# Up projection of a feed-forward block, steps 3 to 10: the weights' high part against both token parts in one 512-column product

## The reference, cut to what matters

```python
D_MODEL, SEQ, FFN_HIDDEN, FFN_CONV = 1024, 256, 2816, 3
...
h = h + merged @ w_out
hid = causal_dwconv(rms_norm(h, ffn_norm_g) @ w_ffn_up, ffn_conv_w, ffn_conv_b)
g_ff, up = jnp.split(hid, 2, axis=-1)
return h + (jax.nn.silu(g_ff) * up) @ w_ffn_down
...
return rms_norm(h, final_norm_g)
```

## Time and profile before

| | us |
|---|---|
| median of 3 runs | 750.46 (750.32 to 751.18) |
| span of the profiled execution | 752.8 |
| TensorE busy in it | 704.3 |
| VectorE busy in it | 529.6 |
| ScalarE busy in it | 345.1 |

### The profile page before, as it was taken

How to read it: one execution, slowest core, us unless ns; L and a number is a source line. 1 busy time by engine, 2 the same in 40 slices (tenths; PEclk the granted TensorE clock), 3 DMA queues, 4 the chain that set the end, 5 groups by cost and what they waited for, 6 DMA issues and landing times.

```text
span 752.8 us, 13896 instructions
## 1 busy us (share of the span) xinstructions
PE 704.3 (94%) x5478; PEld 684.3 (91%) x5478; DVE 529.6 (70%) x614; ACT 345.1 (46%) x397; POOL 98.9 (13%) x56
## 2 busy tenths in 40 slices
PE   5599968979798999999999999999999999999994
PEld 5599967979798999999999999999999999999993
DVE  3789967989967465667664544566559877777784
ACT  5436416445463444544543333443355644555542
POOL 2735320413247000000000000000000000000021
PEclk9889988999999999999999999999999999999998
DMA  8619559464853554334346675655435656555511
GB/s 267 184 47 347 111 85 328 120 211 123 283 180 96 168 167 158 122 119 155 125 161 181 196 237 174 201 183 195 147 133 175 216 177 202 178 171 201 185 56 56
DMA packets 118280, 128.40 MB, mean 171 GB/s; under 512 B 4302, under 2 KB 113263, under 8 KB 117743
## 3 DMA queue, kind: packets, MB, share of 16 engines
q1 hardware_dynamic: 118255, 128.04, 53.9%
HBM read 125.37 MB, written 2.65 MB: 170 GB/s over the span
## 4 chain that ended last, share of the span: by engine, by line
PE 69%; DVE 13%; issue 6%; SPq 5%; POOL 2%; ACT 2%; DMA 2%; DVEq 0%; POOLq 0%; ACTq 0%
PE ps L337 22%; PE ps L338 22%; PE ps L339 22%; DVE conv_a L1169 4%; DVE w_lo L309 3%; SPq L291 3%; DMA w_raw<-w_in 2%; SPq L283 1%; POOL mem_nat L1529 1%; DVE dt_w L1131 1%; DVE conv_g L1439 1%; POOL mem_nat L1531 1%; POOL stat L1486 1%; ACT w_hi L305 1%; PE ps L377 1%
## 5 line engine op out<-in xcount | busy, mean ns | idle before, releaser
L337 PE MATMUL ps<-tok_hi,w_hi 128*128 128x256 f32 x1056 | 306.1, 290 | 6.7 <-DVE w_lo L309 3.6
L338 PE MATMUL ps<-tok_lo,w_hi 128*128 128x256 f32 x1056 | 302.7, 287 | 0.0
L339 PE MATMUL ps<-tok_hi,w_lo 128*128 128x256 f32 x1056 | 302.6, 287 | 0.0
L309 DVE TENSOR_TENSOR w_lo<-w_raw,w_hi 128x2048 fp32r<-128x2048 f32 x102 | 236.7, 2321 | 69.6 <-ACT w_hi L305 69.3
L305 ACT ACTIVATE w_hi<-w_raw 128x2048 fp32r<-128x2048 f32 x108 | 206.0, 1908 | 66.1 <-PE ps L339 48.7
L337 PEld LDWEIGHTS ps<-tok_hi,w_hi 128*128 128x128 f32 x1056 | 207.3, 196 | 9.9 <-issue 5.5
L338 PEld LDWEIGHTS ps<-tok_lo,w_hi 128*128 128x128 f32 x1056 | 207.1, 196 | 0.4
L339 PEld LDWEIGHTS ps<-tok_hi,w_lo 128*128 128x128 f32 x1056 | 206.6, 196 | 0.0
L1169 DVE SCALAR_TENSOR_TENSOR conv_a<-pad_x,cols_conv,conv_a 128x256 f32<-128x256 f32 x72 | 67.2, 999 | 3.4 <-ACT pad_x L873 3.3
L309 POOL TENSOR_TENSOR w_lo<-w_raw,w_hi 128x2048 fp32r<-128x2048 f32 x6 | 28.0, 4673 | 186.4 <-ACT w_hi L305 186.4
L879 ACT ACTIVATE tanh_a<-conv_a 128x512 f32<-128x512 f32 x12 | 7.6, 631 | 72.5 <-DVE conv_a L1169 72.5
(11 more groups left out here) (276 smaller groups left out, 1230.0 us busy)
## 6 DMA issues: line engine op xcount, KB each, us to landing
w_raw<-w_in SPq DMA_DIRECT2D x95, 512.0 KB, 4.8
w_raw<-w_ffn_up SPq DMA_DIRECT2D x44, 512.0 KB, 4.4
w_raw<-w_ffn_down SPq DMA_DIRECT2D x22, 512.0 KB, 4.1
w_raw<-w_mem_kv SPq DMA_DIRECT2D x16, 512.0 KB, 4.1
w_raw<-w_br_ssm SPq DMA_DIRECT2D x16, 512.0 KB, 4.2
acs_b<-acs_d SPq DMA_DIRECT2D x4, 1024.0 KB, 8.1
w_raw<-w_br_attn SPq DMA_DIRECT2D x8, 512.0 KB, 4.6
w_raw<-w_br_mem SPq DMA_DIRECT2D x8, 512.0 KB, 4.0
```

The costliest lines, as they stand in the source:

```text
L309: dve.tensor_tensor(w_lo[:, s, :], w_raw[:, s, :], w_hi[:, s, :].bitcast(F32), ALU.subtract).then_inc(lo_ready[s], 1)
L337: pe.matmul(o, a[0], b[0], start=start, stop=False, **kw)
L338: pe.matmul(o, a[0], b[1], start=False, stop=False, **kw)
L339: return pe.matmul(o, a[1], b[0], start=False, stop=stop, **kw)
```

## The change

From step `F_WIDE` = 3 on, eight of the eleven steps, the up projection is computed otherwise:

- The tokens are scaled once: VectorE multiplies what was turned into banks 4 to 7 by the gain and by `rstd_b` into `normed` (`normalise`, 8 operations of 256 columns). ScalarE makes the high part (`norm_high`, 4 operations of 512 columns) and VectorE the low part (`norm_low`, 4 of 512 columns). Both lie side by side in `hn`, 256 columns of high part and 256 of low part for each depth tile.
- `gemm_wide` takes the place of `gemm_cols`: the high part of the weights meets high and low part of the tokens in one product of 512 columns that fills a whole bank, and the low part of the weights meets the high part of the tokens in one of 256 columns that adds into the bank's second half. The block of a slot now needs two banks, 0 and 1 for the gate and 2 and 3 for up. The result is the sum of a bank's two halves.
- To take a block, ScalarE first copies the second halves of both banks into `pad_g` or `pad_u`, and VectorE then adds the first halves (in place of the product with `rstd_b`).
- `normalise` stands on VectorE behind step 0, `norm_high` on ScalarE behind step 0, `norm_low` on VectorE behind step 1. Steps 1 and 2 are written out and compute as before. As `normalise` reads banks 4 to 7, the four zero products move behind the up block of step 1, with a wait for all 8 operations of `normalise`, ahead of the first down block.

```diff
--- before.py
+++ after.py
@@ -64,6 +64,7 @@
 BIAS_W = 3 * P
 
 RA, RB, RC, RD, RE, RF, RG = 0, 8, 12, 16, 20, 24, 26
+F_WIDE = 3
 
 
 def constants():
@@ -207,6 +208,8 @@
     last_hi = place("last_hi", R + 20, [2, T], F32R)
     last_lo = place("last_lo", R + 22, [2, T], F32R)
     rstd_b = place("rstd_b", R + 18.5, [T])
+    normed = place("normed", R + 72, [KT, T])
+    hn = place("hn", R + 56, [KT, 2, T], F32R)
     pad_g = place("pad_g", R + 0, [2, FTAPS - 1 + T])
     pad_u = place("pad_u", R + 2.25, [2, FTAPS - 1 + T])
     conv_g = place("conv_g", R + 4.5, [2, T])
@@ -268,6 +271,7 @@
     x_again, late_gain, h_sumsq, h_var, h_rstd, h_spread, rstd_b_ready, h_turned, h_hi, h_lo = map(
         sem, ("x_again", "late_gain", "h_sumsq", "h_var", "h_rstd", "h_spread", "rstd_b_ready", "h_turned", "h_hi",
               "h_lo"))
+    n_step, n_hi, n_lo, crossed = map(sem, ("n_step", "n_hi", "n_lo", "crossed"))
     pads_zero, conv_begun, f_step, g_tanh, g_silu, hid_done, hid_hi_s, hid_lo_s = map(
         sem, ("pads_zero", "conv_begun", "f_step", "g_tanh", "g_silu", "hid_done", "hid_hi_s", "hid_lo_s"))
     down_done, y_added, y_sumsq, y_var, y_rstd, y_scaled, y_out = map(
@@ -337,6 +341,24 @@
         pe.matmul(o, a[0], b[0], start=start, stop=False, **kw)
         pe.matmul(o, a[0], b[1], start=False, stop=False, **kw)
         return pe.matmul(o, a[1], b[0], start=False, stop=stop, **kw)
+
+    def gemm_wide(pe, r, s):
+
+        pe.wait_ge(lo_ready[s], r + 2)
+        pe.wait_ge(bank_free[s], r + 1)
+        for j in range(2):
+            b = 2 * s + j
+            for k in range(KT):
+                w = slice(k * CW + j * P, k * CW + (j + 1) * P)
+                if k:
+                    pe.matmul(ps[:, b, T:2 * T], w_lo[:, s, w], hn[:, k, 0, :], start=False, stop=False,
+                              skip_group_check=True)
+                mm = pe.matmul(halves(b), w_hi[:, s, w], hn[:, k, :, :], start=k == 0, stop=k == KT - 1,
+                               skip_group_check=True)
+                if k == 0:
+                    pe.matmul(ps[:, b, T:2 * T], w_lo[:, s, w], hn[:, k, 0, :], start=False, stop=False,
+                              skip_group_check=True)
+        mm.then_inc(gemm_done[s], 1)
 
     def rows_part(pe, s, t, ks, hi, lo, start, stop, **kw):
 
@@ -819,16 +841,32 @@
                         mm = pe.matmul(ps[:, 3, t * P:(t + 1) * P], stat[:, 4 + t:5 + t].to_broadcast([P, P]), ident,
                                        start=True, stop=True)
                     mm.then_inc(h_spread, 1)
-                    for b in range(4, 8):
-                        open_bank(pe, b)
-            with pe.Fori(1, F_STEPS) as f:
-                r = f + (RG - 1)
-                gemm_cols(pe, r, 0, tok_hi, tok_lo)
-                gemm_cols(pe, r, 1, tok_hi, tok_lo)
+
+            def down(r, f):
+
                 pe.wait_ge(hid_lo_s, f)
                 pe.wait_ge(lo_ready[2], r + 2)
                 down_part(pe, 2, 0, hid_hi, hid_lo)
                 down_part(pe, 2, 1, hid_hi, hid_lo).then_inc(gemm_done[2], 1)
+
+            for f in range(1, F_WIDE):
+                r = f + (RG - 1)
+                gemm_cols(pe, r, 0, tok_hi, tok_lo)
+                gemm_cols(pe, r, 1, tok_hi, tok_lo)
+                if f == 1:
+                    pe.wait_ge(n_step, KT)
+                    for b in range(4, 8):
+                        open_bank(pe, b)
+                down(r, f)
+            pe.wait_ge(n_lo, KT // 2)
+            pe.wait_ge(bank_free[1], RG + F_WIDE)
+            pe.wait_ge(bank_free[2], RG + 1)
+            pe.wait_ge(rstd_b_ready, 1)
+            with pe.Fori(F_WIDE, F_STEPS) as f:
+                r = f + (RG - 1)
+                gemm_wide(pe, r, 0)
+                gemm_wide(pe, r, 1)
+                down(r, f)
             pe.wait_ge(hid_lo_s, F_STEPS)
             pe.wait_ge(lo_ready[0], RG + F_STEPS + 1)
             for t in range(NT):
@@ -1026,8 +1064,13 @@
             split_hi(act, RG, 0)
 
 
-            def ffn(f, sa, ra, sb, rb, after_gate, after_up, last, first=False, final=False):
+            def ffn(f, sa, ra, sb, rb, after_gate, after_up, last, first=False, final=False, wide=False):
                 for n, (s, r, pad, conv, tile) in enumerate(((sa, ra, pad_g, conv_g, 0), (sb, rb, pad_u, conv_u, FT))):
+                    if wide:
+                        act.wait_ge(gemm_done[s], r + 1)
+                        act.wait_ge(f_step, 8 * f - 4 + 4 * n)
+                        act.activation(pad[:, :, FTAPS - 1:], ps[:, 2 * s:2 * s + 2, T:2 * T],
+                                       ACT.Copy).then_inc(crossed, 1)
                     act.wait_ge(bank_free[s], r + 2)
                     if not first:
                         act.wait_ge((g_silu, hid_done)[n], f)
@@ -1048,12 +1091,22 @@
                 for rr, ss in last:
                     split_hi(act, rr, ss)
 
+            def norm_high():
+
+                act.wait_ge(n_step, KT)
+                for k in range(0, KT, 2):
+                    act.activation(hn[:, k:k + 2, 0, :], normed[:, k:k + 2, :], ACT.Copy).then_inc(n_hi, 1)
+
             ffn(0, 1, RF + 1, 2, RF + 1, [(RG, 1)], [(RG, 2)], [], first=True)
-            with act.Fori(1, F_STEPS - 1) as f:
+            norm_high()
+            for f in range(1, F_WIDE):
                 r = f + (RG - 1)
                 ffn(f, 0, r, 1, r, [(r + 1, 0)], [(r + 1, 1)], [(r + 1, 2)])
+            with act.Fori(F_WIDE, F_STEPS - 1) as f:
+                r = f + (RG - 1)
+                ffn(f, 0, r, 1, r, [(r + 1, 0)], [(r + 1, 1)], [(r + 1, 2)], wide=True)
             r = RG + F_STEPS - 2
-            ffn(F_STEPS - 1, 0, r, 1, r, [(r + 1, 0)], [], [], final=True)
+            ffn(F_STEPS - 1, 0, r, 1, r, [(r + 1, 0)], [], [], final=True, wide=True)
             for n in range(2 * NT):
                 act.wait_ge(y_added, n + 1)
                 act.activation(h_sc[:, n // 2, halfcols(n)], h_nat[:, n // 2, halfcols(n)], ACT.Square,
@@ -1419,12 +1472,32 @@
             dve.wait_ge(pads_zero, 2)
 
 
-            def ffn(f, sa, ra, sb, rb, early, after_gate, after_up, final=False):
+            def normalise():
+
+                for k in range(KT):
+                    dve.scalar_tensor_tensor(normed[:, k, :], ps[:, 4 + k // 2, (k % 2) * T:(k % 2 + 1) * T],
+                                             cols_gate[:, 5 * KT + k:5 * KT + k + 1], rstd_b[:], ALU.mult,
+                                             ALU.mult).then_inc(n_step, 1)
+
+            def norm_low():
+
+                for k in range(0, KT, 2):
+                    dve.wait_ge(n_hi, k // 2 + 1)
+                    dve.tensor_tensor(hn[:, k:k + 2, 1, :], normed[:, k:k + 2, :], hn[:, k:k + 2, 0, :].bitcast(F32),
+                                      ALU.subtract).then_inc(n_lo, 1)
+
+            def ffn(f, sa, ra, sb, rb, early, after_gate, after_up, final=False, wide=False):
 
                 def pad_with(s, r, pad, splits):
                     dve.wait_ge(gemm_done[s], r + 1)
-                    dve.tensor_tensor(pad[:, :, FTAPS - 1:], halves(s), rstd_b[:].unsqueeze(1).to_broadcast([P, 2, T]),
-                                      ALU.mult).then_inc(bank_free[s], 1)
+                    if wide:
+                        inner = pad[:, :, FTAPS - 1:]
+                        dve.wait_ge(crossed, 2 * (f - F_WIDE) + s + 1)
+                        dve.tensor_tensor(inner, ps[:, 2 * s:2 * s + 2, 0:T], inner, ALU.add).then_inc(bank_free[s], 1)
+                    else:
+                        dve.tensor_tensor(pad[:, :, FTAPS - 1:], halves(s),
+                                          rstd_b[:].unsqueeze(1).to_broadcast([P, 2, T]),
+                                          ALU.mult).then_inc(bank_free[s], 1)
                     for rr, ss in splits:
                         split_lo(dve, rr, ss)
 
@@ -1458,11 +1531,17 @@
                 dve.tensor_tensor(lo[:], hid[:], hi[:].bitcast(F32), ALU.subtract).then_inc(hid_lo_s, 1)
 
             ffn(0, 1, RF + 1, 2, RF + 1, [(RG, 0)], [(RG, 1)], [])
-            with dve.Fori(1, F_STEPS - 1) as f:
+            normalise()
+            for f in range(1, F_WIDE):
                 r = f + (RG - 1)
                 ffn(f, 0, r, 1, r, [(r, 2)], [(r + 1, 0)], [(r + 1, 1)])
+                if f == 1:
+                    norm_low()
+            with dve.Fori(F_WIDE, F_STEPS - 1) as f:
+                r = f + (RG - 1)
+                ffn(f, 0, r, 1, r, [(r, 2)], [(r + 1, 0)], [(r + 1, 1)], wide=True)
             r = RG + F_STEPS - 2
-            ffn(F_STEPS - 1, 0, r, 1, r, [(r, 2)], [], [], final=True)
+            ffn(F_STEPS - 1, 0, r, 1, r, [(r, 2)], [], [], final=True, wide=True)
             for n in range(2 * NT):
                 dve.wait_ge(down_done, n + 1)
                 part = h_nat[:, n // 2, halfcols(n)]
```

## The result

The changed kernel takes 754.97 us (median of 15 runs, 752.93 to 758.18), the one before 751.18 in the 15 runs beside it. The ratio is 1.0047, 95% interval 1.0033 to 1.0060: 3.5 us slower, 2.5 to 4.5. 753.5 (3.0 more) was forecast, put to the 750.46 of the first three runs; the ratio makes 754.0 of them.

What follows compares the result with a forecast made beforehand. TensorE's pace was taken to bound the middle steps, VectorE step 1, and a chain the last step. The terms -3.0 + 3.1 + 2.2 + 0.7 = +3.0 us on 750.46 gave 753.5 us, range 751.6 to 755.9.

Steps and rivals of the forecast that it cites:

- The bound: Whole block: TensorE's pace sets the step at 16.98 us; VectorE is late in step 1, a chain holds the last step.
- (1) Fewer products: TensorE in wide steps: merged products gain 0.40 us a step, 3.0 us in all (bounds 0 and 6.2).
- rival D: Wide steps: narrow products pay no cost of their own, so the body gives 6.2 us, not 3.0; 750.3 us; chance 0.06.
- (2) Handing over: Middle steps: ScalarE's copy ahead of VectorE's addition stays hidden, margin 0.88 us, cost 0.
- (3) Step 1: Scaling on VectorE delays the first down block 2.67 us, `norm_high` adds 0.4; step 2 starts 3.1 us late.
- (4) The last step: Last step's chain: gate copy adds 0.67 us, copy of up behind tanh and later up taps 1.56; in all 2.2 us.
- (5) The clock: Last down projection: idle time of 5.4 us instead of 2.93 lowers TensorE's clock for longer, 0.7 us lost.
- The sum: Whole kernel: -3.0 + 3.1 + 2.2 + 0.7 = +3.0 us, 753.5 us.
- A: Step 1: TensorE's clock falls there as well, 1.7 us more, 755.2 us; chance 0.20.
- B: Wide steps: wide product costs as two narrow, or late copies make steps wait; 3.0 us not gained, 756.5; chance 0.06.
- C: First and last steps: the waits at both ends come out half as long, 750.8 to 751.9 us; chance 0.12.

Runs made afterwards that it cites:

- e4: Changed kernel with each 512-column product cut into two of 256 columns, same banks and handing over; ratio 1.0073 to the kernel before.
- e10: Changed kernel with each of ScalarE's copies made twice, the first into an unused place; one profiled run, +6.3 us against the kernel before, no ratio.
- e9: Changed kernel with VectorE's scaling of the tokens done twice, the first into an unused place; one profiled run, +8.6 us against the kernel before, no ratio.
- e2: Changed kernel with the token scaling moved out of VectorE's way, partly to ScalarE, and wide products from step 4; ratio 0.9996 to the kernel before.
- e6: The changed kernel itself, run again; ratio 1.0044 to the kernel before.
- e1: Changed kernel with the last step computed as before, narrow products and no ScalarE copy; ratio 1.0016 to the kernel before.
- e5: Changed kernel with ScalarE's copy of up made ahead of tanh in the last step alone; ratio 1.0022 to the kernel before.
- e3: Changed kernel with the edits of e1 and e2 together, wide products in steps 4 to 9 alone; ratio 0.9962 to the kernel before.
- e7: Changed kernel with products that nobody reads filling TensorE's wait in step 1; ratio 1.0043 to the kernel before.

## Why the prediction was right

**The bound.** TensorE's pace set the middle steps, and its two waits were at the two ends, as read from the earlier trace rows.

**(1) Fewer products.** Right, and the size by the rows nearly so: 0.35 us a step for 0.40. The pair takes 0.3494 us (11.18 us for 32 of them), 0.002 more than the sum of its two kinds in the kernel before. The bound of 6.2 us, on which rival D rested, has fallen with it: a narrow and a wide product in turn cost what they cost each among its like. A merged pair saves a product and its weight load together; which of the two the 0.011 us belong to, no run tells. By the 2.5 ns that the Trainium skill ("TensorE: Matmul & The Clock Gate", section "Wait — 56ns, not 53.3ns?") has for each of back-to-back products at the full clock, the estimate would have been 0.08 us a step. The rows have 0.35, and e4 puts all of it to the merged product.

**(2) Handing over.** Right at no cost in a middle step: e4 has the handing over and the old step time. The margin worked out as 0.88 us shows in e10, where 1.08 us more cost 0.23. As forecast, tanh starts 11.0 us into the step (709.46 in the trace of after, of step 9 from 698.45), and the low part of the gate weights ends at 15.65 (15.7 in the sum).

**(3) Step 1.** The mechanism and the place as described; e9 and e2 show it from both sides. 2.72 us for 3.1: the first delay was 2.61 (18.38 for 15.77) for 2.67, and the part mis-sized was the second, through ScalarE's `norm_high`, taken as 0.4 us. VectorE's wait for tanh was 0.45 us there, but the low part of the gate weights ended at 581.54, when the down block was just through: it came out as 0.11 us up to the first product of step 2 and 0.10 from that product to the next. The 0.10 isn't the low part of the tokens, which was ready in time: where the clock fell and the down block took longer (e6), step 2 took 16.98 us with the same `norm_low` ahead of it. The first of the two pieces of waiting was 0.32 us and not 0.7. The sum put the four zero products at 0.9, but from their start to the next product are 0.68 (560.78 to 561.46 in the trace of before).

**(4) The last step.** 2.03 us for 2.2; e1 and e5 show where, 0.69 for the gate's copy (0.67 in the sum) and 1.34 for the order on ScalarE (1.56). The 0.86 us taken from a middle step for ScalarE's begin of the up taps was 0.73 here (731.63 to 732.36 in the trace of after).

**(5) The clock.** 0.53 us in the two profiles for 0.7, and that is luck. The sum took it that a longer idle time costs more behind it, and the runs don't bear that out: the same 2.93 us was followed by a fall in the profiles of before and e1 and by none in that of e3; behind 5.14 us the last 24 products took 7.7, 7.2, 6.9 and 7.7 us (after, e2, e6, e7), behind 3.79 us 8.4 (e5) and behind 6.12 us 7.3 (e10), for 7.18 before.

**The sum.** +2.74 for +3.0 is nearer than its parts: 0.36 us too much gained by the products stands against 0.3 us too much lost in step 1 and 0.2 each in the last step and the clock.

**The rivals.** A, given a chance of 0.20, was seen in three (e4, e6, e10) of the six profiles that have the changed kernel's wait in step 1, at 1.6 us; it held in those of after, e1 and e5. As one half of the executions it would add 0.8 to the profiled 2.7 and make the timed 3.5; that is a sum that fits, not a thing shown, since filling the wait (e7) moved the median by nothing that can be told. B is out by the steps of 16.63 us, C by the earlier trace rows and e2, D by the pair.

## What to carry to other kernels

A merged product saves only what each product costs beyond its columns, here 0.011 us for each of the 32 that went, so count what has to be made ready for it and where that stands: here 3.1 us of VectorE in the one step in which VectorE was already late, and a second engine in a chain at the very end where nothing hides it. Look at the first and the last turn of each edit in a loop apart: the changed kernel became one of 0.9962 by leaving the last turn as it was and by moving the preparation, in part to another engine, to times with room (and the wide products to begin one step later). And compare two traces from a point behind the parts that did not change: by their spans alone the slower kernel looked 0.6 us faster.

## What the runs showed of the hardware that was not expected

- The clock can fall in an idle time that is made of two pieces with zero products between them (0.32 and 1.85 us), in three executions of six with the same instructions up to there, and cost 1.6 us each time.
- The last 24 products took 8.4 us behind an idle time of 3.79 us (e5) and 7.3 us behind one of 6.12 us (e10): the longer idle time did not cost more.
- 12 products that nobody reads, put into an idle time of 2.9 us, made the kernel before 2.1 us faster (1.3 to 2.9).
- Executions of the same instructions reached the mark between 557.65 and 561.11 us, which is more than the whole effect of the change.
